# First layer's operand transposed by gate chunk from the unnormed state, with the final norm's factors moved into the next norm

## The reference, cut to what matters

```python
def rms_norm(x, w):
    xf = x.astype(jnp.float32)
    inv = lax.rsqrt(jnp.mean(xf * xf, axis=-1, keepdims=True) + EPS)
    return (xf * inv).astype(x.dtype) * w

# the end of the first block
gate = jax.nn.sigmoid(rms_norm(x, ple_norm_w[i]) @ w_ple_gate[i])
x = x + gate * (p[i] @ w_ple[i])
return rms_norm(x, final_norm_w)
...
# the beginning of the second block, layer 0
h = rmsnorm(x, norm_mix_g[i])
y = short_conv_mixer(h, a_w_in[ia], a_conv_w[ia], a_w_out[ia])
x = x + y
...
def short_conv_mixer(h, w_in, conv_w, w_out):
    b_gate, c_gate, u = jnp.split(h @ w_in, 3, axis=-1)
    return (b_gate * depthwise_conv3(c_gate * u, conv_w)) @ w_out
```

## Time and profile before

| | |
|---|---|
| median of 3 runs | 1985.14 us (1984.21 to 1991.61) |
| the profiled execution | 1989.05 us, of which the span is 1987.2 us |
| PE busy with matmuls | 1914.0 us, 96% of the span |
| DVE, ACT, POOL busy | 1375.7, 920.6 and 46.2 us |
| mean granted TensorE clock | 0.986 of full speed |
| memory traffic | 183 GB/s over the span |

### The profile page before, as it was taken

The page is one execution under the profiler, slowest core; times in us unless marked ns, Lnnn a source line. Parts: engine busy times, 40 slices in busy tenths (PEclk is TensorE's granted clock), DMA queues, the critical chain, the costliest instruction groups (busy, mean ns, idle before and its releaser), DMA issues.

```text
span 1987.2 us, 32582 instructions
## 1 busy us (share of the span) xinstructions
PE 1914.0 (96%) x13424; PEld 1747.6 (88%) x13424; DVE 1375.7 (69%) x1577; ACT 920.6 (46%) x990; POOL 46.2 (2%) x65
## 2 busy tenths in 40 slices
PE   6999998999999979999999999999988999999999
PEld 6998888788888779999989899987878999999998
DVE  5777974876777676766667566677997666676665
ACT  4544842755666553443345353334344333434332
POOL 0000000000000000001101000000000000000000
PEclk9999998999999989999999999999999999999999
DMA  7552351887787647555553386552324555555553
GB/s 226 174 172 92 122 162 63 312 307 271 283 306 297 255 141 191 186 191 191 194 181 111 107 239 202 191 189 86 106 70 145 191 193 196 176 181 183 190 190 106
DMA packets 243915, 366.03 MB, mean 184 GB/s; under 512 B 12566, under 2 KB 217961, under 8 KB 231401
## 3 DMA queue, kind: packets, MB, share of 16 engines
q1 hardware_dynamic: 243817, 364.64, 54.6%
HBM read 363.57 MB, written 1.05 MB: 183 GB/s over the span
## 4 chain that ended last, share of the span: by engine, by line
PE 73%; DVE 8%; issue 2%; ACT 1%; DMA 1%; DVEq 0%; POOL 0%; SPq 0%; ACTq 0%
PE proj L958 34%; PE acc L1292 11%; PE proj L1477 10%; PE proj L977 6%; PE acc L1445 5%; DVE ring_lo L2455 1%; PE acc L1305 1%; PE acc L1553 1%; PE proj L1745 1%; PE acc L1677 1%; PE acc L1002 1%; PE proj L1584 1%; ACT ring_hi L1893 0%; DVE ring_lo L3142 0%; PE misc L1426 0%
## 5 line engine op out<-in xcount | busy, mean ns | idle before, releaser
L2455 DVE TENSOR_TENSOR ring_lo<-raw,ring_hi 128x2048 fp32r<-128x2048 f32 x242 | 560.1, 2317 | 216.2 <-ACT ring_hi L1893 215.1
L1893 ACT ACTIVATE ring_hi<-raw 128x2048 fp32r<-128x2048 f32 x242 | 462.3, 1914 | 448.9 <-PE proj L958 210.8
L958 PE MATMUL proj<-h_hi,ring_hi 128*128 128x256 f32 x1424 | 408.8, 287 | 7.8 <-DVE ring_lo L2455 7.6
L958 PE MATMUL proj<-h_lo,ring_hi 128*128 128x256 f32 x1424 | 397.0, 279 | 0.0
L958 PE MATMUL proj<-h_hi,ring_lo 128*128 128x256 f32 x1424 | 396.8, 279 | 0.0
L958 PE MATMUL proj<-g_hi,ring_hi 128*128 128x256 f32 x1088 | 304.6, 280 | 1.2 <-DVE g_lo L2499 1.2
L958 PE MATMUL proj<-g_lo,ring_hi 128*128 128x256 f32 x1088 | 303.4, 279 | 0.0
L958 PE MATMUL proj<-g_hi,ring_lo 128*128 128x256 f32 x1088 | 303.3, 279 | 0.0
L958 PEld LDWEIGHTS proj<-h_hi,ring_hi 128*128 128x128 f32 x1424 | 269.1, 189 | 19.9 <-issue 9.8
L958 PEld LDWEIGHTS proj<-h_lo,ring_hi 128*128 128x128 f32 x1424 | 269.7, 189 | 4.1 <-issue 3.1
L958 PEld LDWEIGHTS proj<-h_hi,ring_lo 128*128 128x128 f32 x1424 | 268.9, 189 | 0.0
(11 more groups left out here) (445 smaller groups left out, 3459.4 us busy)
## 6 DMA issues: line engine op xcount, KB each, us to landing
raw<-in_f_w_dram SPq DMA_DIRECT2D x132, 1024.0 KB, 5.1
raw<-in_w_in_dram SPq DMA_DIRECT2D x29, 1024.0 KB, 5.4
raw<-in_w_exp_gate_dram SPq DMA_DIRECT2D x25, 1024.0 KB, 5.3
raw<-in_w_exp_up_dram SPq DMA_DIRECT2D x24, 1024.0 KB, 5.0
raw<-in_a_w_in_dram SPq DMA_DIRECT2D x24, 1024.0 KB, 5.2
raw<-in_w_exp_down_dram SPq DMA_DIRECT2D x23, 1024.0 KB, 6.1
raw<-in_b_w_qkv_dram SPq DMA_DIRECT2D x12, 1024.0 KB, 5.1
raw<-in_c_w_in_dram SPq DMA_DIRECT2D x12, 1024.0 KB, 5.1
```

The lines of the kernel that those rows point to most:

```text
L958: last = pe.matmul(bank[:, a, :], w[:, k, a * P:(a + 1) * P], h[:, k, :], start=(k == 0 and w is hi and h is h_h and (a == 0 or not first) ...
L1893: act.activation(w_hi[n.slot][:, :], raw[n.slot][:, :], ACT.Copy).then_inc(hi_ready, 1)
L2455: dve.tensor_tensor(w_lo[n.slot][:, :], raw[n.slot][:, :], w_hi[n.slot][:, :].bitcast(f32), SUB)\
```

## The change

It has five parts. (1) `turns("mix0")` makes the transposes of the operand `mix0` behind chunks 1, 2 and 3 of `ple_gate`, from x as it is before the final norm, each group when the addition to its columns is done. ACT and DVE take their parts of the operand between their `ple_gate` work, and DVE's four final-norm operations now wait until all transposes have read x. (2) Since those columns lack the final norm's weight, DVE multiplies the first 8 columns of `norm_mix_g_2` in `params` by those of `final_norm_w`, once at the start; for this `final_norm_w` is loaded as 8 further parameter rows, by a 15th DMA. (3) They lack the token factor too: POOL keeps the final norm's factor (`inv_final`) and multiplies the next norm's by it, a copy and a multiplication more. (4) `spread_inv("mix0")` stands behind chunk 1 of `a_c0` and no longer behind chunk 0. (5) On ACT the squares of `mix0` follow each other behind the chunk's high part, with no operand work between them.

```diff
--- before.py
+++ after.py
@@ -124,7 +124,7 @@
 
 PARAMS = [("attn_norm_w", 8), ("moe_norm_w", 8), ("ple_norm_w", 8), ("ssd_norm_w", 8),
           ("conv_w", 40), ("conv_b", 10), ("norm_mix_g_2", 32), ("norm_ffn_g_2", 32),
-          ("a_conv_w_2", 48), ("c_short_w_2", 72), ("c_short_b_2", 24), ("c_f_skip_2", 16)]
+          ("a_conv_w_2", 48), ("c_short_w_2", 72), ("c_short_b_2", 24), ("c_f_skip_2", 16), ("final_norm_w", 8)]
 ROW = {}
 _c = 0
 for _name, _n in PARAMS:
@@ -354,6 +354,7 @@
         ssq = sb("ssq", [P, TT, 2])
         ms = sb("ms", [P, TT])
         inv = sb("inv", [P, TT])
+        inv_final = sb("inv_final", [P, TT])
         neg_half = sb("neg_half", [P, 16])
         eps_col = sb("eps_col", [P, 1])
         h_hi = sb("h_hi", [P, KT, SEQ], f32r)
@@ -661,6 +662,9 @@
         def state_of(operand):
             return "ple" if operand == "final" else NORMS[NORM_OF[operand]][1]
 
+        def turned_state(operand):
+            return "ple" if operand == "mix0" else state_of(operand)
+
         def wait_x(eng, state, kk, t):
 
             if state == "input":
@@ -996,7 +1000,7 @@
             def turn(operand, kk, halves=range(TT)):
 
                 for t in halves:
-                    wait_x(pe, state_of(operand), kk, t)
+                    wait_x(pe, turned_state(operand), kk, t)
                     for a in range(2):
                         k = 2 * kk + a
                         last = pe.transpose(turn_bank(operand, kk)[:, a, t * P:(t + 1) * P],
@@ -1818,10 +1822,8 @@
             sort_tokens()
             experts()
             unsort("ple")
-            project("ple_gate", product_t, "ple")
-            for kk in range(KT // 2):
-                turn("mix0", kk)
-            project("a_c0", product_f, "mix0", {0: lambda: spread_inv("mix0")})
+            project("ple_gate", product_t, "ple", turns("mix0"))
+            project("a_c0", product_f, "mix0", {1: lambda: spread_inv("mix0")})
             project("a_u0", product_f, "mix0")
             project("a_b0", product_f, "mix0")
             project("a_out0", product_t, "conv0", turns("ffn0"))
@@ -1848,7 +1850,14 @@
                 pool.wait_ge(ssq_ready, 4 * (n + 1))
                 chain.link(pool.tensor_tensor(ms[:, :], ssq[:, :, 0], ssq[:, :, 1], ADD))
                 chain.link(pool.tensor_scalar(ms[:, :], ms[:, :], 1.0 / D, EPS, MUL, ADD))
-                pool.tensor_tensor(inv[:, :], ms[:, :], neg_half[:, 0:TT], POW).then_inc(inv_ready, 1)
+                if operand == "mix0":
+                    chain.link(pool.tensor_tensor(ms[:, :], ms[:, :], neg_half[:, 0:TT], POW))
+                    pool.tensor_tensor(inv[:, :], ms[:, :], inv_final[:, :], MUL).then_inc(inv_ready, 1)
+                else:
+                    pool.tensor_tensor(inv[:, :], ms[:, :], neg_half[:, 0:TT], POW).then_inc(inv_ready, 1)
+                if operand == "final":
+                    pool.wait_ge(inv_ready, n + 1)
+                    chain.link(pool.tensor_copy(inv_final[:, :], inv[:, :]))
                 if operand in SPREAD:
                     pool.wait_ge(inv_ready, n + 1)
                     pool.tensor_tensor(inv_diag[:, :, :], ident[:, :].unsqueeze(1).to_broadcast([P, TT, P]),
@@ -2248,11 +2257,15 @@
                     act.activation(gate_s[:, t, :], pair(s.slot)[:, t, :], ACT.Sigmoid, scale=inv[:, t:t + 1]).then_inc(gate_sig, 1)
                 if not in_norm("ple_gate", j):
                     part(s)
+                if j:
+                    high_turned("mix0", j - 1)
                 if j == 2:
                     squares("final", 0)
+            high_turned("mix0", 3)
             squares("final", 1)
             part(last_chunk(BEFORE["final"]))
-            norm_quarters("mix0")
+            squares("mix0", 0)
+            squares("mix0", 1)
             parts("a_c0")
             parts("a_u0", short_conv(0), urgent=True)
             parts("a_b0")
@@ -2548,6 +2561,8 @@
             dve.wait_ge(params_ready, 1)
             for kk in range(KT // 2):
                 low_turned("attn", kk)
+            mix_cols, final_cols = [params[:, ROW[n]:ROW[n] + KT] for n in ("norm_mix_g_2", "final_norm_w")]
+            link(dve.tensor_tensor(mix_cols, mix_cols, final_cols, MUL))
             norm_end("attn")
             for c in range(RING):
                 low(Chunk(c))
@@ -3224,8 +3239,10 @@
                 link(dve.tensor_tensor(gate_m[:, :, :], gate_s[:, :, :],
                                        ple_y[:, :].rearrange("p (t n) -> p t n", t=TT)[:, :, ds(j * COLS, COLS)], MUL))
                 return dve.tensor_tensor(xs, xs, gate_m[:, :, :], ADD)
-            drain("ple_gate", add_ple)
+            drain("ple_gate", add_ple, {1: lambda: low_turned("mix0", 0), 2: lambda: low_turned("mix0", 1),
+                                        3: lambda: (low_turned("mix0", 2), low_turned("mix0", 3))})
             dve.wait_ge(drained, DRAINED["ple_gate"] + FIRST["ple_gate"][1])
+            dve.wait_ge(turned, (NORM_OF["mix0"] + 1) * (KT // 2))
             dve.wait_ge(late_tables, 16 * LATE_DMAS)
             dve.wait_ge(inv_ready, SQUARED.index("final") + 1)
             for t, m in QUARTERS:
@@ -3233,8 +3250,6 @@
                 dve.scalar_tensor_tensor(out=x[:, t, cols], in0=x[:, t, cols], scalar=inv[:, t:t + 1], in1=final_w[:, cols],
                                          op0=MUL, op1=MUL).then_inc(x_quarter, 1)
             part(last_chunk(BEFORE["final"]))
-            for kk in range(KT // 2):
-                low_turned("mix0", kk)
             norm_end("mix0")
             spread("mix0")
             link(dve.tensor_tensor(inv_b2[:, :], inv_b[:, :], inv_b[:, :], MUL))
```

## The result

The changed kernel takes **2011.54 us** (2009.69 to 2011.93, 4 runs), the kernel before, run beside it, 1986.05 us (1984.21 to 1991.61, 4 runs). The ratio is 1.0127, 95% interval 1.0114 to 1.0139: 1.3% slower, where 1977.5 us and no case above 1989.4 had been named. The profiled execution took 2011.15 us, its span is 2009.3 us. All medians and ratios here leave out two executions that took far longer than the others of their kernel, one of e14 (2557.16 us at a mean granted clock of 0.699) and one of the kernel before beside e5 to e8 (3849.49 us).

A forecast was written before the change was run, and what follows sets the result against it. PE, busy 96%, was taken to bound the kernel, leaving only its idle places and low-clock stretches. Handover 9.7 less clock fall 1.7 less start 0.4 gave 7.6 us off the median 1985.14: 1977.5 us, range 1972.5 to 1982.5.

The forecast's parts named there:

- The handover, 9.7 us: From `ple_gate` to `a_c0`: chunk 0 ends at 741.85 instead of 751.57, a gain of 9.7 us at full clock.
- the 0.7 for the two calls inside `ple_gate`: Two transpose calls now inside `ple_gate`'s full stream cost PE 0.35 us each, 0.7 us together.
- The clock: Some 2 us of PE idle time before the last transposes bring the clock down, costing 1.7 us; the rival: no fall.
- the rows of 363 and 1514: Profile rows around these times: PE idle for 1.91 and 1.66 us with the clock at 1.00 throughout.
- that of 1453: Profile row around this time: 2.17 us of PE idle time, followed by the low clock level.
- The start, 0.4 us: At kernel start DVE's new product and the 15th DMA delay PE's first product, 0.4 us together.
- The factor: POOL's token factor is ready at 747.3, PE asks at 747.5, 0.2 us spare; rival, late: 1981 us, chance 0.07.
- The slow pace: Rival: the new handover brings the slower matmul pace to 11 chunks, 2.4 us lost, 1979.9 us; chance 0.15.
- "No cost": Behind the spread in `a_c0`: only drains queue behind DVE's wait, and PE first asks for them at chunk 3; 0 us.
- The sum: Whole kernel: 8.0 us from handover and clock less 0.4 for the start, 7.6 us faster, 1977.5 us; chance 0.40.
- the worst of them, by falls of the clock: Rival: behind 736 us up to seven other idle times lose the clock, 1.7 us each, up to 1989.4 us; chance 0.05.
- clock kept: Rival: PE keeps its clock through the new handover, 9.3 us gained in all, 1975.8 us; chance 0.33.

The follow-up runs named there:

- e14: e4 with 96 unused bytes a partition behind the factors, operands 96 bytes farther from the rings: 2001.27 us, 1.0072.
- e5: The kernel before with an unused tile ahead of the rings, so that everything moves by 32 bytes: 1984.70 us, 0.9987.
- e8: The kernel before with 128 unused bytes behind `inv`, moving every later tile by 128: 2010.34 us, 1.0113.
- e1: The changed kernel with `inv` and `inv_final` in one tile, all other addresses as in the kernel before: 1979.55 us, 0.9972.
- e4: e1 with the four bias transfers spread over `a_u0` and `a_b0`, the first behind chunk 1: 1978.59 us, 0.9968.
- e2: The kernel before with an unused 8-byte tile behind `inv`, moving every later tile by 32 bytes: 2014.45 us, 1.0149.
- e6: The kernel before with an unused tile behind `inv_b`, moving only the work region by 32 bytes: 2010.39 us, 1.0114.
- e7: The kernel before with `ms` moved behind `inv_b`, so that only `h_hi` to `inv_b` move down by 32 bytes: 2001.06 us, 1.0032.
- e12: The kernel before with only the four attention bias loads spread over `a_u0` and `a_b0`: 1986.87 us, 1.0003.
- e3: The kernel before with 64 unused bytes behind `inv`, moving every later tile by 64: 2024.13 us, 1.0198.
- e9: e1 with part 4 undone, the spread behind chunk 0 of `a_c0` again: 1985.10 us, 0.9995.
- e13: e4 with `ident_sb` ahead of `h_hi` and `inv_b` ahead of the rings, `h` 512 bytes farther, work region 1024 nearer: 1977.60 us, 0.9958.
- e10: e4 with five small tiles ahead of the rings, operands 192 bytes nearer to the rings: 2015.52 us, 1.0147.

## Why the prediction was wrong

**The handover, 9.7 us: right against this profile, in part by luck.** From the end of `ple_gate` to the end of chunk 0 it was 751.57 - 732.52 = 19.05 us; in the changed kernel it is 3.08 + 5.68 = 8.76. The difference of 10.3, less the 0.7 for the two calls inside `ple_gate`, is 9.6. e1 and e4, lined up with the kernel before, gain 9.1 us between 700 and 760. But 2.2 of it rest on the execution that was profiled before. In all eight profiled kernels that have the old handover the clock falls while PE stands idle for 6.02 us. In five (e2, e5, e6, e7, e12) it is back before the first product of `a_c0`, and the next 8 us have a granted clock of 1.00; in three (the kernel before, e3, e8) these have 0.71, 0.71 and 0.79. e12's first chunk took 5.74 us and e5's 5.91, not 7.99. Against such an execution the handover gives some 7.4 us (an estimate: 9.6 less 7.99 - 5.74). The prediction took the one row of 7.99 for what every execution has.

**The clock: the rival was right.** I took a fall for 1.7 us; behind 2.00 us of idle time the stretch shows 1.00. In all nine profiled kernels with the new handover the clock was kept there, with the rows of 363 and 1514 and against that of 1453. Behind e9's wait of 5.2 us it fell. The Trainium skill (TensorE: Matmul & The Clock Gate, "HAM oscillation — how this bites in real kernels") had it kept here, and the traces agree at this place.

**The start, 0.4 us: it cost nothing that shows.** PE's wait for the last parameter row ended at 11.98 (12.13 before) and the first product came at 19.82 (20.21 before). DVE's new product of 128x8 took 0.16 us, as estimated.

**The factor: right.** POOL's first operation was held for 1.36 us until DVE's low part ended, and the copy into `inv_final` was not held (it began 0.07 us ahead of DVE's first final-norm operation). By the Trainium skill (SBUF — State Buffer, "SBUF: two separate sides") DVE with two inputs and a GpSimd operation that reads exclude each other; the trace agrees at this place, since the 1.36 us end when the low part does. The factor was ready 0.8 us before PE wanted it. Part 4 is needed: e9 shows the 5.2 us.

**The slow pace: it came, but not by the new handover alone.** Chain of waits behind the spread, in the kernel before and then in e4:

```profile
752.00 58.05 PE proj L958 x512
```

```profile
735.44 10.90 PE proj L962 x96
...
746.77 53.24 PE proj L962 x452
```

58.05 / 512 = 113.4 ns before; in e4 53.24 / 452 = 117.8 behind the spread, and 113.3 from start to start in the second chunk, just ahead of it. e4 is 10.2 us ahead of the kernel before at 760 and 8.3 at 860. So the 2.4 us of the rival came, as 1.9. But the new handover isn't needed for it: e12, with the old handover and with nothing changed but the place of the bias loads, runs this stage at 117.8 too (above), and so do e1, e4, e9 and e13, while e5 has 113.4 like the kernel before. In layer 3 the same stages run at 117.8 in the kernel before, e1 and e4, and at 113.3 in e5, e9, e12 and e13. All have the same distances, or those of e13, and full clock. What sets the pace stays open, and with one profile a kernel no run shows whether it is the kernel's or the execution's.

**"No cost" behind the drains: wrong by 2.2 us.** The step said that only the drains are queued behind DVE's wait for the spread, and that PE asks for the first of them at chunk 3. It left out SP, which stands at `load_bias` until that drain, with the weights of `a_u0` behind it. Against PE's first matmul of `a_c0` it goes on 3.6 us later than before (13.7 for 10.1).

**The sum: the step that failed.** It counted instructions, waits and clock, and took the pace of every other matmul as given. The tile `inv_final` stood in the sum only as a copy of POOL's. Its place in the allocation was worth +28.4 us in the profiled execution (changed against e1), four times the gain. None of the rivals was this mechanism, and the worst of them, by falls of the clock, ended 22 us too low. The balance of the profiled executions: forecast -7.6; clock kept -1.7; start -0.4; turns and handover +0.1; stall +2.2; slow pace +1.9. That makes -5.5, where e1's span is 6.3 us below that of the kernel before. This is what the balance can be tested by; the +28.4 for the addresses is itself the difference to e1, and with it the sum is +22.9, measured 2009.3 - 1987.2 = +22.1.

**The version to keep** is the change with its two factors in one tile and with the bias loads spread (e4: 0.9968, 0.9957 to 0.9980), or e13 of the same distances modulo 256 (0.9958, 0.9944 to 0.9972). Both are faster than both kernels; between the two the intervals don't decide.

## What to carry to other kernels

Where a change adds, removes or resizes a tile, compare the addresses of all tiles behind it before any time is compared: if the pace of untouched matmuls differs, first give the addresses back (here by sharing a slot, e1; a tile behind all the fixed ones still moved the work region, e6), and only then judge the change. Read the pace as start to start of ten matmuls in a full stream that the change doesn't touch, or as the busy time of a large group: 3.5 ns in 7536 matmuls are 26 us. Take two or three profiles of the kernel before, too: one execution's low clock or slow stage is easily read as a cost that the change removes. And when a drain is made to wait, look up who else waits for that drain, load queues included.

## What the runs showed of the hardware that I had not expected

- At full clock, with nothing waiting, a 128x128 by 128x256 matmul started each 113 ns in the quick stages of the kernel before and each 118 ns with 32 bytes more between `h_hi` and the rings. With 64 more it was 120 ns: in e3's timeline the matmuls at 62.29 and 63.49 are ten apart. Moving both by 32 bytes does nothing (e5), and e3 and e10 agree at 256 bytes from each other. Through which access this comes about, no run shows.
- With the very same distances there are still two paces, 113.4 and 117.8 ns, that last for 50 us and more and change at a place like the spread (e4). The same stage of kernels with the same distances takes the one or the other (113.4 in e5, 117.8 in e12).
- With PE idle for 6.02 us in the old handover, the clock fell in all eight profiles, and in three of them the low level reached into the next stage and cost some 2 us there (7.99 us for the first chunk, 5.74 in e12).
- Beside four transfers of 438 KB one of the 1 MB loads took 16.89 us in the chain, from its issue to ACT's start; the median of these loads from issue to landing is 5.1 us in the page. With the four spread out (e4) ACT waited for no load in that stretch.
